# Five instead of four seven-product pairs in the second column pair of an MLP turn, and a new order of products in the first such pair

## What is computed

```python
h2 = rmsnorm(x, norm2_g[l])
x = x + jnp.square(jax.nn.relu(h2 @ w_up[l])) @ w_down[l]
```

## Time and profile before

| | before |
|---|---|
| median of 3 runs | 2036.02 us (2035.47 to 2036.15) |
| the profiled execution | 2035.84 us |
| its span from first to last instruction | 2034.0 us |
| PE / DVE / ACT / POOL busy share of the span | 100% / 73% / 59% / 11% |
| granted TensorE clock, mean | 1.000 |
| HBM read | 377.95 MB, 187 GB/s |

### The profile page before, as it was taken

The page is one execution under the profiler, slowest core; times in us unless marked ns, Lnnn a source line. Parts: engine busy times, 40 slices in busy tenths (PEclk is TensorE's granted clock), DMA queues, the critical chain, the costliest instruction groups (busy, mean ns, idle before and its releaser), DMA issues.

```text
span 2034.0 us, 27169 instructions
## 1 busy us (share of the span) xinstructions
PE 2028.2 (100%) x10602; PEld 1702.3 (84%) x10602; DVE 1482.5 (73%) x1917; ACT 1190.1 (59%) x1572; POOL 225.7 (11%) x228
## 2 busy tenths in 40 slices
PE   9999999999999999999999999999999999999999
PEld 7887788888888888888888877888888888888887
DVE  7767556688679668868777775666886796697685
ACT  6557644566466457556545576445655664575563
POOL 6254100000000000002023531000000000000000
PEclk9999999999999999999999999999999999999999
DMA  9477966677667676767654678666776786777674
GB/s 302 130 230 191 233 183 185 185 216 230 188 197 241 196 201 211 225 187 202 205 175 144 218 199 225 188 184 188 227 216 187 201 241 194 202 215 220 189 212 130
DMA packets 182815, 411.35 MB, mean 202 GB/s; under 512 B 14122, under 2 KB 22800, under 8 KB 182688
## 3 DMA queue, kind: packets, MB, share of 16 engines
q1 hardware_dynamic: 173968, 379.52, 61.1%
q0 software_dynamic: 8544, 30.01, 8.3%
q10 hardware_dynamic: 176, 0.09, 0.0%
HBM read 377.95 MB, written 2.12 MB: 187 GB/s over the span
## 4 chain that ended last, share of the span: by engine, by line
PE 99%; DVE 0%; issue 0%; ACT 0%; DVEq 0%
PE psum L636 23%; PE psum L612 21%; PE psum L639 12%; PE psum L616 10%; PE psum L679 10%; PE psum L682 5%; PE psum L646 3%; PE psum L647 3%; PE psum L650 3%; PE psum L729 2%; PE psum L730 2%; PE psum L733 2%; PE psum L744 1%; PE psum L818 1%; PE psum L797 0%; PE psum L843 0%
## 5 line engine op out<-in xcount | busy, mean ns | idle before, releaser
L941 ACT CAST w_hi<-raw_ring 128x1024 fp32r<-128x1024 f32 (+1 forms) x720 | 743.7, 1041 | 711.3 <-PE psum L639 319.6
L1182 DVE TENSOR_TENSOR w_lo<-raw_ring,w_hi 128x1024 fp32r<-128x1024 f32 (+1 forms) x664 | 811.6, 1230 | 422.0 <-ACT w_hi L941 420.2
L636 PE MATMUL psum<-xt,w_hi 128*128 128x512 f32 x2048 | 513.3, 392 | 0.3 <-issue 0.3
L636 PEld LDWEIGHTS psum<-xt,w_hi 128*128 128x128 f32 x2048 | 368.7, 189 | 67.0 <-issue 0.7
L639 PEld LDWEIGHTS psum<-xt,w_lo 128*128 128x128 f32 x2048 | 279.4, 190 | 20.0
L639 PE MATMUL psum<-xt,w_lo 128*128 128x256 f32 x2048 | 285.6, 282 | 0.0
L612 PE MATMUL psum<-w_hi,xt 128*128 128x512 f32 (+1 forms) x1152 | 281.5, 386 | 0.3 <-ACT w_hi L941 0.3
L612 PEld LDWEIGHTS psum<-w_hi,xt 128*128 128x128 f32 x1152 | 202.4, 188 | 41.2 <-issue 2.7
L679 PE MATMUL psum<-w_hi,ht_lo 128*128 128x512 f32 x448 | 174.4, 389 | 0.0
L679 PE MATMUL psum<-w_hi,ht_hi 128*128 128x512 f32 x448 | 174.4, 389 | 0.0
L1738 POOL DMA_DIRECT2D lo_own<-raw_ring x28 | 24.2, 865 | 1184.7 <-ACT lo_own L957 1184.7
(11 more groups left out here) (210 smaller groups left out, 2451.8 us busy)
## 6 DMA issues: line engine op xcount, KB each, us to landing
raw_ring<-in_w_up_dram SPq DMA_DIRECT2D x256, 512.0 KB, 3.9
raw_ring<-in_w_down_dram SPq DMA_DIRECT2D x256, 512.0 KB, 4.7
raw_ring<-in_w_in_dram SPq DMA_DIRECT2D x128, 512.0 KB, 4.7
raw_ring<-in_w_out_dram SPq DMA_DIRECT2D x64, 512.0 KB, 4.9
w_lo<-raw_ring POOLq DMA_DIRECT2D x28, 512.0 KB, 6.3
lo_own<-raw_ring POOLq DMA_DIRECT2D x28, 512.0 KB, 5.9
raw_ring<-in_w_in_dram SPq DMA_DIRECT2D x16, 256.0 KB, 2.9
x<-in_x_dram SPq DMA_DIRECT2D x8, 256.0 KB, 7.3
```

The costliest lines, as they stand in the source:

```text
L636: pe.matmul(bank[:, f, :], w_hi[:, w, j, f * P:(f + 1) * P], both, start=kt == 0, stop=False, skip_group_check=True)
L941: act.copy(w_hi[:, u % AHEAD, :, 0:cols], raw_ring[:, u % RAWS, :, 0:cols]).then_inc(hi_ready, 1)
L1182: dve.tensor_tensor(w_lo[:, u % AHEAD, :, 0:cols], raw_ring[:, u % RAWS, :, 0:cols], w_hi[:, u % AHEAD, :, 0:cols].bitcast(F32), ALU.subtr ...
```

## The change

The list `SEVEN_AT` gives the positions of seven-product pairs for each column pair, and `ORDER` which pair of row blocks stands at a position. For d = 0 both are as before. For d = 1 the order is 0, 1, 2, 3, 5, 4, 6, 7 and the seven-product pairs stand at positions 1, 3, 4, 6, 7. Pair 6 (`EXTRA`) is new among them, and has its own tiles of hidden sums, `extra_hi` and `extra_lo`. The second of two neighbours is one that `follows_seven`: its `t_hi` and `t_lo` are made two units later in the queues of ACT and DVE, ahead of the split of unit u + 3, and its first sums come straight behind the `t_lo` of the pair before it. The summed unit B.8 becomes B.10. `swap` now holds for the first seven-product pair of both column pairs, and the wait for `evicted[0]` moves into own(). In the last pair of d = 1 the product of quarter (1, 0) is no longer finished ahead of the other two.

```diff
+EXTRA = 6
+ORDER = [tuple(range(KPS)), (0, 1, 2, 3, 5, 4, EXTRA, 7)]
+SEVEN_AT = [(1, 3, 5, 7), (1, 3, 4, 6, 7)]
...
-SUMMED_PAIR = [LOOP0 + LOOP_UNITS * i + 16 * d + m for i in range(LOOPS) for d in range(2) for m in (0, 8)]
+SUMMED_PAIR = [LOOP0 + LOOP_UNITS * i + m for i in range(LOOPS) for m in (0, 8, 16, 26)]
...
+        def follows_seven(pl, u):
+
+            return seven_at(pl, u) is not None and seven_at(pl, u - 2) is not None
...
@@ PE: seven_products
-                if first and d == 0:
-                    pe.wait_ge(evicted[0], pl.evictions(18))
-                swap = last or first and d == 1
+                if kp == EXTRA:
+                    pe.wait_ge(extra_done, pl.l * LOOPS + pl.i + 1)
+                swap = last or first
...
                 def own():
+                    if first and d == 0:
+                        pe.wait_ge(evicted[0], pl.evictions(18))
                     if first and d == 1:
                         pe.wait_ge(totals_out, pl.l * TURNS + pl.i + 1)
...
-                if last:
+                if last and d == 0:
                     bank, of, t, _ = products.pop(0)
...
-                for bank, (a_hi, a_lo), t, start in products:
+                for n, (bank, (a_hi, a_lo), t, start) in enumerate(products):
                     mm = pe.matmul(bank, a_hi, t_lo[:, t, :], start=False, stop=True, skip_group_check=True)
+                    if last and d == 1 and n == 0:
+                        mm.then_inc(pair_done, 1)
                 mm.then_inc(sevens_done, 1)
@@ ACT: split_hi
                 act.wait_ge(unit_done, pl.unit(u + 1))
+                if follows_seven(pl, u - 2) and seven_at(pl, u - 2)[0] == 1:
+                    t_hi_of(seven_at(pl, u - 2)[1])
...
-                if seven is not None and seven[0] == 1:
-                    act.wait_ge(t_raw_ready, seven[1] + 1)
-                    if seven[1]:
-                        act.wait_ge(sevens_done, seven[1])
-                    act.copy(t_hi[:, :, :], t_raw[:, :, :]).then_inc(t_hi_ready, 1)
+                if seven is not None and seven[0] == 1 and not follows_seven(pl, u):
+                    t_hi_of(seven[1])
@@ ACT: activations
+                if part == "pair" and c == 0 and k == 6 and pl.i < LOOPS:
+                    act.wait_ge(extra_raw, pl.l * LOOPS + pl.i + 1)
+                    act.copy(extra_hi[:, :, :], s_raw[:, 0, :, :]).then_inc(extra_cast, 1)
@@ DVE: split_lo
+                if follows_seven(pl, u - 2) and seven_at(pl, u - 2)[0] == 1:
+                    t_lo_of(seven_at(pl, u - 2)[1])
+                after, seven = seven_at(pl, u + 1), seven_at(pl, u)
+                if after is not None and after[0] == 0 and seven is None:
                     first_sums(pl, u + 1)
...
                 dve.tensor_tensor(w_lo[:, u % AHEAD, :, 0:cols], raw_ring[:, u % RAWS, :, 0:cols],
                                   w_hi[:, u % AHEAD, :, 0:cols].bitcast(F32), ALU.subtract).then_inc(split_done, 1)
+                if seven is not None and seven[0] == 1:
+                    if pair_at(pl, u)[1:] == (1, 2 * SEVEN_AT[1][0] + 1):
+                        take_totals(pl, pair_at(pl, u)[0])
+                    if not follows_seven(pl, u):
+                        t_lo_of(seven[1])
+                    if after is not None:
+                        first_sums(pl, u + 1)
                 if after is not None and after[0] == 0:
                     dve.wait_ge(t1_ready, after[1] + 1)
                     dve.tensor_tensor(t_raw[:, 1, :], raw_ring[:, (u + 2) % RAWS, 1, :], raw_ring[:, (u + 1) % RAWS, 1, :],
                                       ALU.subtract).then_inc(t2_ready, 1)
@@ DVE: mlp
+                if part == "pair" and c == 0 and k == 5 and pl.i < LOOPS:
+                    dve.wait_ge(s_done, pl.l * 2 * TURNS + 2 * pl.i + 2)
+                    sums_of(slice(EXTRA % 4, EXTRA % 4 + 1), 1, extra_raw)
+                if part == "pair" and c == 0 and k == 7 and pl.i < LOOPS:
+                    dve.wait_ge(extra_cast, pl.l * LOOPS + pl.i + 1)
+                    dve.tensor_tensor(extra_lo[:, :, :], s_raw[:, 0, :, :], extra_hi[:, :, :].bitcast(F32), ALU.subtract).then_inc(extra_done, 1)
```

More of the change, by code:

```diff
@@ L78 @@
 BLOCKS = {b: [kp % 4 for kp in SEVEN if kp // 4 == b] for b in range(2)}
-SEVENS = (LOOPS * 2 + 1) * len(SEVEN)
+EXTRA = 6
+ORDER = [tuple(range(KPS)), (0, 1, 2, 3, 5, 4, EXTRA, 7)]
+SEVEN_AT = [(1, 3, 5, 7), (1, 3, 4, 6, 7)]
+TURN_SEVENS = sum(len(at) for at in SEVEN_AT)
+SEVENS = LOOPS * TURN_SEVENS + len(SEVEN_AT[0])
 BANK_MOVES = (2 * LOOPS + 1) * 4
@@ L202, in encoder @@
         w_lo = sb("w_lo", [P, AHEAD, 2, CW], F32R)
+        with ExitStack() as extra:
+            extra_hi, extra_lo = [extra.enter_context(nc.sbuf_tensor(f"extra_{h}", [P, 4, P], F32R)) for h in ("hi", "lo")]
         head_in = sb("head_in", [P, RT * CW])
@@ L441, in seven_at @@
             at = pair_at(pl, u)
-            if at is None or at[2] // 2 not in SEVEN:
+            if at is None or at[2] // 2 not in SEVEN_AT[at[1]]:
                 return None
             turn, d, m = at
-            return m % 2, pl.l * SEVENS + (2 * turn + d) * len(SEVEN) + SEVEN.index(m // 2)
+            return m % 2, pl.l * SEVENS + turn * TURN_SEVENS + d * len(SEVEN_AT[0]) + SEVEN_AT[d].index(m // 2)
+        def follows_seven(pl, u):
+            return seven_at(pl, u) is not None and seven_at(pl, u - 2) is not None
         def moves(pl, d):
@@ L451, in sevens_after @@
         def sevens_after(pl, d):
-            return pl.l * SEVENS + (2 * pl.i + d + 1) * len(SEVEN)
+            return pl.l * SEVENS + pl.i * TURN_SEVENS + sum(len(SEVEN_AT[e]) for e in range(d + 1))
         def k_blocks(kp):
@@ L542, in load_pair @@
                 raw_is_free(pl, u)
-                row = turn * D + k_blocks(m // 2)[m % 2] * P
+                row = turn * D + k_blocks(ORDER[d][m // 2])[m % 2] * P
                 sp.dma_start(raw_ring[:, u % RAWS, :, :].rearrange("p j n -> p (j n)"),
@@ L664, in pair_steps @@
             def pair_steps(pl, s, d, m):
-                kp, half = m // 2, m % 2
+                kp, half = ORDER[d][m // 2], m % 2
                 a, b = k_blocks(kp)
@@ L685, in seven_products @@
             def seven_products(pl, s, d, kp, a, b):
-                i, first, last = SEVEN.index(kp), kp == SEVEN[0], kp == KPS - 1
+                first, last = kp == SEVEN[0], kp == KPS - 1
                 _, number = seven_at(pl, s)
@@ L690, in seven_products @@
                     pe.wait_ge(s_done, pl.l * 2 * TURNS + 2 * pl.i + kp // 4 + 1)
[L691 to L693 removed]
+                if kp == EXTRA:
+                    pe.wait_ge(extra_done, pl.l * LOOPS + pl.i + 1)
+                swap = last or first
                 def s_tile(n):
[L696 removed]
+                    if kp == EXTRA:
+                        return [t[:, n, :] for t in (extra_hi, extra_lo)]
+                    return [t[:, SEVEN.index(kp), n, :] for t in (s_hi, s_lo)]
                 def own():
+                    if first and d == 0:
+                        pe.wait_ge(evicted[0], pl.evictions(18))
                     if first and d == 1:
@@ L941, in split_hi, with t_hi_of @@
                 act.copy(w_hi[:, u % AHEAD, :, 0:cols], raw_ring[:, u % RAWS, :, 0:cols]).then_inc(hi_ready, 1)
-                if seven is not None and seven[0] == 1:
-                    act.wait_ge(t_raw_ready, seven[1] + 1)
-                    if seven[1]:
-                        act.wait_ge(sevens_done, seven[1])
-                    act.copy(t_hi[:, :, :], t_raw[:, :, :]).then_inc(t_hi_ready, 1)
+                if seven is not None and seven[0] == 1 and not follows_seven(pl, u):
+                    t_hi_of(seven[1])
                 if is_summed(pl, u) and not has_own_lo(pl, u):
                     act.activation(w_lo[:, u % AHEAD, :, :], raw_ring[:, u % RAWS, :, :], ACT.Copy, scale=-1.0).then_inc(lo_negated, 1)
+            def t_hi_of(number):
+                act.wait_ge(t_raw_ready, number + 1)
+                if number:
+                    act.wait_ge(sevens_done, number)
+                act.copy(t_hi[:, :, :], t_raw[:, :, :]).then_inc(t_hi_ready, 1)
             def negate_ahead(pl, u):
@@ L1187, in split_lo, with t_lo_of @@
                                       ALU.subtract).then_inc(t2_ready, 1)
[L1188 to L1192, removed]
+            def t_lo_of(number):
+                dve.wait_ge(t_hi_ready, number + 1)
+                dve.tensor_tensor(t_lo[:, :, :], t_raw[:, :, :], t_hi[:, :, :].bitcast(F32), ALU.subtract).then_inc(t_lo_ready, 1)
             def first_sums(pl, u):
@@ L1207, in token_sums, with sums_of @@
                 own, _, nb = s_places(b)
-                fs = slice(own.start - 8 * b, own.stop - 8 * b, own.step)
+                sums_of(slice(own.start - 8 * b, own.stop - 8 * b, own.step), nb, s_raw_ready)
+            def sums_of(fs, nb, ready):
                 a1, a2 = (t[:, :].rearrange("p (f q) -> p f q", f=4)[:, fs, :] for t in mlp_t)
```

(4 more changed lines are left out.)

8 lines of the change are left out of this document (2 added, 6 removed).

## The result

The changed kernel takes 2041.6 us (median of 7 runs, 2041.19 to 2043.41) beside 2036.15 us for the kernel before (7 runs): a ratio of 1.0028, 95% interval 1.0019 to 1.0037, so 5.5 us slower. Its profiled execution took 2042.09 us, with a span of 2040.3 us instead of 2034.0.

A forecast was written before the change was run, and what follows sets the result against it. PE's matmuls bound the kernel, with DVE 4.25 us ahead at unit B.15. Six turns of 1.34 - 0.32 = 1.02 us and two last phases of -0.32 gave +5.5 us: 2041.5 us, range 2037.8 to 2044.6.

The forecast's parts named there:

- The stall at a turn's start: PE's wait at L646 in a turn's first seven-product pair: the new order removes 0.32 us, 8 times.
- DVE's chain: Second column pair: DVE's added sums and `t_lo` move the end of B.15's low part from 32.04 to 37.69 us.
- the lead of 4.25: Second column pair, kernel before: DVE finishes B.15's low part 4.25 us before PE asks for it; the change spends this.
- The stall: Each second column pair: PE stalls 2.03 us waiting for DVE at position 7, about 0.3 of it earlier at position 4.
- The first column pair: New sums, cast and low part make unit A.15 1.80 us late, hidden with 0.02 + 0.12 us to spare; cost 0.
- The sum: Whole kernel: six turns of +1.02 us and two last pair phases of -0.32 us give +5.5 us, 2041.5 us.
- Hidden work: Rival: DVE's additions fit in its lead in the second column pair, PE keeps all 6.6 us: 2029.4 us; chance 0.10.
- A wait of DVE for its own result: Rival: such waits cost nothing, so 0.44 + 0.24 us leave DVE's chain in the second column pair: 2037.4 us; chance 0.12.
- the 0.22 behind a `t_lo`: DVE, second column pair: sums straight behind a `t_lo` wait for its result, 1.88 instead of 1.66 us; 0.44 in all.
- The price of wide sums: Rival: first column pair has no cover; wide-sum prices cost 0.4 us in each of 6 turns, up to 2044.5; chance 0.13.
- the last quarter's copy: Same rival of chance 0.13: ACT's copy before the up phase, margin 0.1 us, costs as much as the wide sums.
- The clock: Rival: PE's clock falls to 1.2 GHz in the stall, 4.3 us more for 19 matmuls, six times: 2067; chance 0.02.

The follow-up runs named there:

- e1: Kernel before with only the new order of products in the first seven-product pair of d = 0: 2032.64 us, ratio 0.9986.
- e7: Kernel before with five more 128x1024 additions (6.3 us) on DVE behind the `t_lo` of position 5 of d = 1: 2047.88 us.
- e3: Changed kernel with DVE's sum of the totals in turns 1 and 2 cut to 32 of 512 columns per bank: 2037.62 us, single run.
- e4: e2 with the `t_hi` of position 4 cast ahead of unit B.10 on ACT instead of B.11: 2031.32 us, ratio 0.9980 to the kernel before.
- e8: Changed kernel with one more 128x512 addition (0.60 us) on DVE behind the new sums' low part in the first column pair: 2045.51 us, single run.
- e5: Changed kernel with the third sum at positions 4 and 7 taking a wrong operand, so DVE needs no wait there: 2041.01 us, single run.
- e2: Changed kernel with the last pair of d = 1 doing its first unit, B.14, first: 2036.58 us, ratio 1.0005 to the kernel before.

## Why the prediction was right

- **The stall at a turn's start** was put at 0.32 us, 8 times. The column pairs lost 0.32 to 0.37, and e1 shows it alone.
- **DVE's chain** was to end unit B.15 at 37.69; it ended at 37.72. Of its terms, the sums straight behind a `t_lo` (1.88) and the 0.72 behind a wait came as read; the `t_lo` of position 4 started at 22.98, where 22.97 had been worked out. (The row gives 0.76 of idle time from an end to a start; counted from start to start, as the prediction did, it is 0.84 beside 0.85.) e7 gives the lead of 4.25 as 4.26. The path was right too: DVE's sum in place, three casts, `t_hi`, `t_lo`. What the prediction didn't say is how near the next bound on it stood: e3 and e4 show that the single buffer of `t_hi` takes over when `t_hi` comes 0.8 us sooner, so that 2.0 us less of work on DVE bring 0.77.
- **The stall** was to be 2.03 us, about 0.3 at position 4. It was 42.21 - 177 x 0.2268 = 2.07, with 0.32 at position 4 and 1.62 at position 7; the rest is in distances at most 0.03 longer than usual, the first of them where PE waits for the totals at position 1. One thing was left unsaid: of what I called a wait for `w_lo` at position 7, 0.36 + 0.11 us come first as a wait for ACT's cast of B.15, itself held up by DVE's sum in place for position 7. It is part of the same lateness, and changes no sum.
- **The first column pair** was to hide 1.80 us with 0.02 + 0.12 to spare. The low part behind the new sums started 29.04 after the column pair's start, 27.25 before: 1.79. e8 gives the margin as 0.13. The new sums and the `t_lo` behind them lie as worked out (`t_lo` 26.77 after the column pair's start, where 26.78 was to be):

```profile
443.19 0.28 DVE L1245 TENSOR_TENSOR s_raw<-head_in,head_sq 128x128 f32<-128x128 f32 x1
443.51 0.29 DVE L1246 TENSOR_TENSOR s_raw<-head_in 128x128 f32<-128x128 f32 x1
443.72 0.28 DVE L1247 TENSOR_TENSOR s_raw<-s_raw,head_in 128x128 f32<-128x128 f32 x1
...
447.36 1.76 DVE L1222 TENSOR_TENSOR t_lo<-t_raw,t_hi 128x1536 fp32r<-128x1536 f32 x1 [0.15 <-ACT t_hi L967]
```

- **The sum** of +5.5 us came out as 5.5 by the medians. That it fits to 0.1 is partly luck, since single executions differ by more; the terms fit to some hundredths in each turn, and these repeat.
- **The rivals.** Hidden work fell with the result, and e7 shows why: the same DVE that is busy 73% of the span has 4.3 us of room here. A wait of DVE for its own result costs 0.11 us (e5); the 0.22 behind a `t_lo` came back in all three places of the new order (1.88 or 1.89 from start to start), but no run isolates them. The price of wide sums was not paid: the 128-wide sums were 0.32 and 0.21 apart, as worked out. Nor was that of the last quarter's copy: the up phase behind a second column pair takes as long as before. The clock stayed at 1.00, 2.4 GHz, with 1.27 us from one matmul to the next, and with 1.92 in e7.

By the Trainium skill's rule (VectorE: DVE Perf Modes, "The DRAIN you can't avoid") the semaphore between two operations costs nothing extra; the page measured it on a chain of copies. In e5 the distances of otherwise equal neighbours are 0.61 without and 0.72 with a wait, so the measurement decides against it for operations of 128x512 in float32. The Trainium skill's warning that an idle PE falls to half its clock (TensorE: Matmul & The Clock Gate, "Part 1: The HAM clock gate") found no case here: the granted clock stayed at 1.00 in the column pair of e7 with its 1.92 us between two matmuls.

## What to carry to other kernels

Where one engine is busy all the time, price a change that trades its work for another engine's by that engine's lead at the moment at which its result is asked for, not by its share of busy time: 3.8 us were free here and 6.3 cost 1.9. Then look for what ties the helper, and for the bound behind that one. Here a cast stood behind three others in ACT's queue, and one place sooner took 0.77 us out of the chain. Then the single buffer that PE frees took over, and 2.0 us less of work on DVE had brought the same 0.77. And ask for the operand that is ready first; after each such step, ask again what is late next.

## What was not expected

- e2 gained 0.25 us a turn less than worked out, because a `t_lo` that had 0.8 us to spare behind a long stall had none once the stall was shorter.
- At position 4 PE shows less than 0.1 us of idle time, and the loss is 0.32: the matmuls are drawn 0.39 long at a distance of 0.23. And each stall is followed by one more distance of 0.34, which makes 0.11 us of the price.
- The totals of the first column pair cost up to 0.14 us a turn more in e8. In the kernels before and after they cost 0.04 at most.
